# Half of the channel sums of squares on GpSimd: folding six pieces to three ahead of TensorE

## What is computed

```python
mix = jnp.concatenate([rms_norm(y_conv, g_grp[:D_CONV]),
                       rms_norm(y_attn, g_grp[D_CONV:D_CONV + D_ATTN]),
                       rms_norm(y_gmlp, g_grp[D_CONV + D_ATTN:])], axis=-1)
x = x + jnp.einsum('bse,ed->bsd', mix, w_out)
```

## Time and profile before

| | us |
|---|---|
| median of 3 runs | 2408.57 |
| lowest and highest run | 2406.03, 2411.61 |
| the profiled execution's own time | 2422.95 |
| its span on the core | 2420.9 |
| granted clock of TensorE over the span, share of full | 0.984 |
| TensorE busy | 2332.8 |
| VectorE busy | 1275.0 |
| ScalarE busy | 818.0 |
| GpSimd busy | 119.7 |

### The profile page before, as it was taken

One profiled execution on the slowest core, in us unless ns is written; L12 is line 12 of the kernel. 1 busy time (PEld: TensorE's weight loads), 2 busy tenths in 40 slices (PEclk: granted clock), 3 DMA queues, 4 the chain that ended last, 5 costly groups with the idle time before them and its releaser, 6 DMA issues. The chain is left out here.

```text
span 2420.9 us, 32181 instructions
## 1 busy us (share of the span) xinstructions
PE 2332.8 (96%) x12710; PEld 2078.4 (86%) x12710; DVE 1275.0 (53%) x2205; ACT 818.0 (34%) x1697; POOL 119.7 (5%) x223
## 2 busy tenths in 40 slices
PE   6999999999999989999989989999999999999997
PEld 6987878999999968888888878789999998788885
DVE  4326865443343366765752467663343343766766
ACT  4123422444444422122331244234444443222222
POOL 4010000000000000000020100010000000000001
PEclk9999999999999999999999999999999999999998
DMA  5111001355555586556220110114555557666462
GB/s 158 44 32 43 19 31 44 105 183 208 187 207 206 206 320 261 212 202 246 96 69 27 32 44 19 43 36 152 196 185 209 184 192 285 254 255 261 165 238 119
DMA packets 190374, 361.67 MB, mean 149 GB/s; under 512 B 13308, under 2 KB 96800, under 8 KB 190224
## 3 DMA queue, kind: packets, MB, share of 16 engines
q1 hardware_dynamic: 186368, 352.33, 40.0%
q0 software_dynamic: 2704, 3.10, 0.6%
q10 hardware_dynamic: 1152, 4.19, 0.5%
HBM read 228.01 MB, written 131.37 MB: 148 GB/s over the span
## 5 line engine op out<-in xcount | busy, mean ns | idle before, releaser
L1505 PE MATMUL ps<-hT_hi,w_hi 128*128 128x384 f32 x1824 | 622.1, 341 | 2.7 <-DVE x L1170 2.7
L1507 PE MATMUL ps<-hT_hi,w_lo 128*128 128x384 f32 x1824 | 620.4, 340 | 0.0
L1506 PE MATMUL ps<-hT_lo,w_hi 128*128 128x384 f32 x1824 | 620.2, 340 | 0.0
L1505 PE MATMUL ps<-w_hi,ring 128*128 128x512 f32 x896 | 353.4, 394 | 6.8 <-DVE w_lo L1273 5.7
L1506 PE MATMUL ps<-w_lo,ring 128*128 128x512 f32 x896 | 354.8, 396 | 0.0
L1507 PE MATMUL ps<-w_hi,ring 128*128 128x512 f32 x896 | 352.1, 393 | 0.0
L1505 PEld LDWEIGHTS ps<-hT_hi,w_hi 128*128 128x128 f32 x1824 | 344.2, 189 | 3.2 <-DVE x L1170 3.1
L1506 PEld LDWEIGHTS ps<-hT_lo,w_hi 128*128 128x128 f32 x1824 | 344.1, 189 | 0.0
L1507 PEld LDWEIGHTS ps<-hT_hi,w_lo 128*128 128x128 f32 x1824 | 343.9, 189 | 0.0
L1015 DVE TENSOR_TENSOR w_lo<-w_raw,w_hi 128x512 fp32r<-128x512 f32 (+1 forms) x232 | 143.3, 667 | 324.9 <-ACT w_hi L679 324.8
L1505 PE MATMUL ps<-w_hi,hT_hi 128*128 128x512 f32 (+1 forms) x720 | 279.5, 388 | 8.6 <-ACT vn L866 4.5
(11 more groups left out here) (205 smaller groups left out, 2683.4 us busy)
## 6 DMA issues: line engine op xcount, KB each, us to landing
ff_ops<-row_op SPq DMA_DIRECT2D x224, 512.0 KB, 3.9
ring<-ff_ops SPq DMA_DIRECT2D x56, 2048.0 KB, 8.2
w_raw<-in_w_ff SPq DMA_DIRECT2D x128, 256.0 KB
b<-in_w_ff SPq DMA_DIRECT2D x24, 1024.0 KB, 14.6
w_raw<-in_w_in SPq DMA_DIRECT2D x56, 256.0 KB
w_raw<-in_w_out SPq DMA_DIRECT2D x32, 256.0 KB
ff_last<-last_op SPq DMA_DIRECT2D x32, 256.0 KB, 4.2
w_raw<-in_w_ff SPq DMA_DIRECT2D x8, 1024.0 KB, 10.4
```

What stands on the lines that cost most here:

```text
L1505: pe.matmul(out, sh, mh, start=first, stop=False)
L1506: pe.matmul(out, sh, ml, start=False, stop=False)
L1507: return pe.matmul(out, sl, mh, start=False, stop=last)
```

## The change

GpSimd gets a new instruction for each tile ahead of its power: it waits for the squares of the tile and adds three pieces of 128 columns to the other three, in place (128 partitions x 384 elements). A new semaphore `sq_folded` tells TensorE. ScalarE writes the squares in another order, so that the pieces that are added belong to the same group: the two of `yc` to places 0 and 3, the four of attention to places 1, 2, 4 and 5. `group_sums` then has three matmuls instead of six: piece 0 for column 0, pieces 1 and 2 for column 1. The matmul count falls by 3 x 9 x 2 = 54. What `values` and the next squares wait for is unchanged.

```diff
+        sq_folded = sig("sq_folded")
...
                 for t in range(T):
+                    pool.wait_ge(*sq_done.at(t))
+                    nc.gpsimd.tensor_tensor(sq6[:, 0:3, :], sq6[:, 0:3, :], sq6[:, 3:6, :],
+                                            ALU.add).then_inc(*sq_folded.tick(t))
                     pool.wait_ge(*sg_done.at(t))
...
-                        nc.scalar.activation(sq6[:, 0:2, :], yc[:, :, tile(t)], ACT.Square).then_inc(
+                        sq = sq6[:].rearrange("p (b s) n -> p b s n", b=2)
+                        nc.scalar.activation(sq[:, :, 0, :], yc[:, :, tile(t)], ACT.Square).then_inc(
                             *sq_done.tick((t, 0)))
                         act.wait_ge(*yat_done.at(t))
-                        nc.scalar.activation(sq6[:, 2:6, :], ps[:, 7, :].rearrange("p (h n) -> p h n", h=G4),
+                        nc.scalar.activation(sq[:, :, 1:3, :], ps[:, 7, :].rearrange("p (b s n) -> p b s n", b=2, s=2),
                                              ACT.Square).then_inc(*sq_done.tick(t))
...
             def group_sums(t):
-                pe.wait_ge(*sq_done.at(t))
+                pe.wait_ge(*sq_folded.at(t))
                 if t >= 1:
                     pe.wait_ge(*sg_done.at(t - 1))
-                for col, ks in ((0, range(0, 2)), (1, range(2, 6))):
+                for col, ks in ((0, (0,)), (1, (1, 2))):
```

## The result

The changed kernel is slower. Its median is 2417.63 us over 9 runs (2415.5 to 2427.08), that of the kernel before 2410.0 us over 9 runs (2406.03 to 2411.61). The ratio is 1.0042, with a 95% interval of 1.0027 to 1.0056. The forecast was 2411.6 us and most likely no measurable change; the difference came out at 7.6 us where 3.1 us was forecast.

The account below looks back on a forecast made before the run. TensorE, busy for 96% of the span, bounds the kernel, with VectorE as full in the last turn. Per layer -1.89 + 0.45 - 0.63 + 1.90 + 1.7 = +1.53 us, for both +3.1: 2411.6 us, range 2403 to 2420 us.

Parts of the forecast that it names:

- +1.53 us: Whole change per layer: loop gain, port delay, tail and clock summed; +3.1 us for both layers.
- the clock's term: Tail: longer waits bring one more stretch at 1.2 GHz for each layer, +1.7 us, between none and three.
- the port: Last loop turn: the fold beside VectorE's split of the weights delays VectorE's dense chain, +0.45 us per layer.
- the wait at tile 8: Tail: power and fold stand between `sg` of tile 7 and the sums, +1.73 us; wait about 4.1 us.
- What is removed: Channel sums on TensorE: half of each group of twelve matmuls goes, 0.63 us a group, 11.3 us over 18 groups.
- The fold's length: GpSimd's fold of 128 x 384 for each tile: 0.9 us, between 0.66 and 1.2 us.
- I take half: Port delay at the split in the last turn: half of the range from 0 to 0.9 us, +0.45 us.
- the 2.1 us of idle time: Earlier loop turns: VectorE has 2.1 us of idle time to hide the fold's port delay.
- the dense chain: VectorE, last turn: work from the maximum to the scores of tile 8; only tiles 0 to 2 gain, -1.89 us.
- a lower bound of zero: Port delay at VectorE's split: least value 0, since the split took 2.48 us with and without a GpSimd instruction.
- The queue: GpSimd's list in the tail: fold behind the previous tile's power; TensorE waits for both, tail end +1.90 us late.
- the clock decides: Rival: longer waits at three places per layer each bring a 1.2 GHz stretch, +4.9 us per layer, 2418.5 us; chance 0.30.

Follow-up runs that it names:

- three_only: Changed kernel without the GpSimd fold, three matmuls straight after the squares (half of the channels left out): 2399.61 us, ratio 0.9965.
- fold_ahead: Changed kernel with the fold of tile t+1 ahead of the power of tile t in GpSimd's list: 2403.52 us, ratio 0.9971.
- six_after_fold: Changed kernel with all six matmuls back, behind the fold (pieces 3 to 5 counted twice): 2426.82 us, ratio 1.0079.
- late_sums: GpSimd's fold ahead of the previous tile's power, and sums of tiles 6 and 8 behind the next side rows, against the changed kernel: 2394.88 us, ratio 0.9947.
- filled_short: Changed kernel with 15, 11 and 19 needless matmuls ahead of the scores of tile 8 and the sums of tiles 6 and 8: 2404.39 us, ratio 0.9978.
- fold_narrow: Changed kernel with a fold of one column in place of 128 in each piece: 2410.86 us, ratio 1.0005.
- before_late: Kernel before (six matmuls, no fold) with the sums of tiles 6 and 8 moved behind side rows: 2400.54 us, ratio 0.997.
- after_late: Changed kernel with the sums of tiles 6 and 8 moved behind side rows, GpSimd's order untouched: 2404.25 us, ratio 0.9988.
- late_filled: late_sums with 12 needless matmuls ahead of the scores of tile 8: 2389.31 us, ratio 0.9906.

## Why the prediction was wrong, by its own steps

Per layer the prediction had +1.53 us. Regrouped, that is 9 x 0.63 = 5.7 us of removed matmuls, 5.5 us of longer waits, and 1.7 us of clock. The traces show 9 x 0.67 = 6.0 us removed, the waits up by 7.0 us (3.88 + 7.7 in the changed kernel, the waits at all sums together, against 1.35 + 3.2), and a layer that loses 4.9 us. What is left for the clock is 4.9 + 6.0 - 7.0 = 3.9 us. The milestones say the same without the remainder. From the sums of tile 6 to those of tile 7 it takes 10.94 us after and 8.20 before; less 0.20 us of wait and with the 0.67 us of the group, that is 3.2 us for the new stretch at the lower level. From the sums of tile 8 to the end, 67.52 + 0.67 - 67.59 = 0.6 us come on top. The step that failed is thus the size of the clock's term, **"I count one more such stretch for each layer, +1.7 us"**, and beside it two smaller ones, the port and the wait at tile 8.

- **What is removed: right.** 0.67 us a group where 0.63 was read, turns of 10.6 us. `three_only` shows -2.01 us at the scores of tile 8 where -1.89 was forecast, and the sums of tiles 3 and 4 worth nothing there.
- **The fold's length: close.** 0.99 us in the tail where 0.9 was taken. The estimate of 0.84 us in proportion, from the Trainium skill, GPSIMD Engine Reference, section 3.1, was low by 0.15 us.
- **The port: mis-sized by 0.7 us.** The term was +0.45 us; the runs show 1.17 us. Two steps failed. "I take half" was 0.81 us at the split. And the 2.1 us of idle time in which VectorE was to hide the port in the earlier turns do not lie where they are needed. In turn 7 the fold of 282.25 to 283.25 fell on the rotation, the rotation ended 0.76 us late, and behind it stands the very maximum with which the dense chain starts; only 0.43 us of idle time stood there to take it up. The unchanged length of the split under the power, which I read as a lower bound of zero, said little about a fold that reads 768 elements. The rule of the Trainium skill, SBUF — State Buffer, "SBUF: two separate sides", that such instructions exclude each other for a whole instruction, agrees with these rows: VectorE's rotation ended 0.14 us after the fold.
- **The queue: right in kind, 0.7 us too small.** The wait at tile 6 grew by 1.83 us (forecast 1.73), at tile 7 by 0.20 us (0.32), at tile 8 by 2.40 us (1.73). `fold_ahead` shows that it is this order that costs. The error is at tile 8: the prediction let `sg` of tile 7 move with TensorE, but `three_only` shows that the shorter group of tile 7 brings it no sooner, and 0.67 us of wait come instead.
- **The clock: mis-sized by 2.2 us a layer, the largest error.** There was a stretch at the sums of tile 6 that wasn't there before, of 3.4 us of full clock and not 1.7, and the one at tile 8 was twice as long. Granted clock over the 65 us: 0.92 before, 0.84 after, so 65 x 0.08 = 5.2 us of full clock gone, of which the part under a wait costs nothing: from 342.0 to 344.36 TensorE waited at the lower level, 1.2 us of full clock. The 4.0 us left agree with the 3.9. The rival "the clock decides", with +4.9 us a layer and 2418.5 us, came out nearest. That it met the 4.9 us is luck in part: it had 5.1 us of clock from three new stretches, where there were 3.9 us from one new and one longer one, none of it at the scores; port and queue made up the difference.

Waits 1.5 us too small, clock 2.2 us too small, removed matmuls 0.3 us too small: together 3.4 us a layer, 6.8 us in all. That is why the forecast ended on no change and the kernel moved to the slow side. The price of the clock could have been read better from the trace. The prediction took it from the stretch behind the wait of 2.40 us, 1.7 us. Behind the wait of 1.35 us at the scores the same trace has one of 3.4 us, which the prediction doesn't mention. With both in view, lengthening two waits to 2.6 and 4.1 us made several us of clock a layer the likeliest case and not a rival.

## What to carry to other kernels

An instruction given to an idle engine goes to the end of that engine's list: look at what the one ahead of it waits for, and write the new one ahead of it if its own inputs come first. On a kernel that TensorE bounds, a wait can cost more than its length, by the clock's fall behind it. In the tails traced here a fall of 1.7 to 5.1 us of full clock followed most waits of 1.35 us and more and, with one exception in `six_after_fold`, none of the shorter ones. A longer wait did not always bring a longer fall. Useful work moved there gives both back (`late_sums`); needless matmuls of the right length give back the clock alone (`filled_short`). A fold of 1.0 us on GpSimd held VectorE's two-input instructions up by about 0.8 us in both places looked at, so ask which chain they are in, not whether VectorE has idle time on average.

## What the runs showed of the hardware

**Two paces of the same matmuls at the same clock.** In the MLP, TensorE is busy without a gap at full granted clock in every trace, but starts either 568 or 579 matmuls in 100 us. The first trace of before, and then the same kernel again:

```profile
600.00:700.00 100.00, 100.00 (x568) 1.00 0.53 193
```

```profile
600.00:700.00 100.00, 100.00 (x579) 1.00 0.55 200
```

From the common point of one layer to that of the next the slower pace takes 1419.20 - 224.97 = 1194.23 us, the faster 1411.23 - 226.54 = 1184.69 us: 9.5 us. Of the fourteen traces, the first of before shows 568 in both layers and `fold_narrow` in layer 0 alone (568, then 579). Thus it belongs to no kernel, and can change within an execution.

> The kernel before once more. The pace theory (two paces of the MLP's matmuls, chosen anew by an execution or a load of the program, whatever the kernel) expects that this trace shows 579 matmuls in 100 us of the MLP, as the other five traces do, and not 568, a span near 2408 us, and the attention stage with the same times to a tenth of a us as in the first trace of before. If the pace belongs to the kernel before, it shows 568 again.

Measured: 2407.15 us (10 runs), ratio 0.9999 (0.9983 to 1.0016), span 2406.0 us, 579 matmuls. It explains the 14.9 us between the two traces of the same kernel for the most part, and fits the spread of its runs (2401.5 to 2422.9 us over all occasions). What sets the pace stays open. For a reader of profiles it means that the span of one trace couldn't carry this kernel's difference of 0.3%, while the milestones inside the stage repeated to 0.2 us in these two traces.

**The same meeting on the port can end in two ways.** In turn 8 GpSimd's power starts 0.17 us behind VectorE's split. In most layers it then takes 1.24 us, and in the changed kernel the fold behind it stretches the split to 3.29 us. In four of the 28 layers traced (one each of `six_after_fold`, `before_late`, `after_late` and `late_filled`) the power took 3.5 us and the split stayed at 2.49. The second layer of `after_late`:

```profile
1476.28 2.49 DVE L1020 TENSOR_TENSOR w_lo<-w_raw,w_hi 128x512 fp32r<-128x512 f32 x4
1476.45 3.51 POOL L659 TENSOR_TENSOR rG<-sg,nhalf 128x3 f32<-128x3 f32 x1 [8.74 <-DVE sg L1400]
```

The fold then comes behind the split and delays nothing on VectorE. In `six_after_fold` and `after_late` the other layer went the usual way, and there the scores of tile 8 come 0.8 us later (77.19 against 77.99 in `six_after_fold`, 75.54 against 76.33 in `after_late`). What decides between the two ways stays open.

**A power of three elements costs nearly as much as a sum of 384.** On GpSimd the power over 128x3 took 0.85 us, the fold over 128x384 0.99 us, an add over 128x3 0.20 us.
